# A hybrid encoder layer on one core: SSD moved under the pointwise and gated products, attention on its own

## The chip, the cores and the metric

One core of one Trainium2 chip. The metric is the device time of one execution in microseconds, the median of several runs. A profiled execution on the same chip gives the trace that is read below. Its engines are called PE (TensorE, matrix products), DVE (VectorE), ACT (ScalarE), POOL (GpSimd) and SP (SyncE, which issues nearly all DMAs).

## What is computed

One layer over 1088 tokens (1024 of a new stream, 64 of a running one), width 1024, all in float32. The input is normalised and projected; four mixers work on parts of the projection; their outputs are joined and projected back; a mixture of experts follows, and a last norm.

```python
def _layer(x, p, st, is_prompt):
    xn = _rmsnorm(x, p['g_mix'])
    proj = xn @ p['w_in']
    u_a, u_b, u_c, u_d = jnp.split(proj, [...], axis=-1)
    y_c, k_new, v_new = _band_attention_prompt(u_c, p['att_rel_bias'])   # or _sample, with a cache
    y_a, ssd_conv, ssd = _ssd_mixer(u_a, st['ssd_conv'], st['ssd'], p)   # a recurrence over tokens
    y_b, ccm_conv = _conv_module(u_b, st['ccm_conv'], p)                 # 31 taps, norm, pointwise product
    y_d, s5_re, s5_im = _s5_mixer(u_d, st['s5_re'], st['s5_im'], p)      # ends in ga * sigmoid(gb)
    mixed = jnp.concatenate([y_a, y_b, y_c, y_d], axis=-1) @ p['w_out']
    h = x + mixed
    return h + _hier_moe(_rmsnorm(h, p['g_ffn'])), ...                   # 32 experts, two for each token
```

## The kernel before, in words

The program is one list of instructions for each engine, in an order written out by hand; semaphores join them. An engine runs its list in order, so an instruction that waits holds up everything behind it on its engine. Tokens lie in 9 chunks of 128 (the last has 64). A float32 product runs as two passes through PE, so a product over one 512-column piece shows as two matmuls in the trace.

- **Projection** (`tile_part`, L603): 16 tiles of 128 output channels, two accumulators psA and psB in turn, 8 inner steps k. A pass covers 1088 tokens in the pieces of `CH` (L301): 512, 512 and 64, since a PSUM bank holds 512. ACT or DVE evacuates a finished tile into the arenas (L1123 to L1150, `gate_moved` L1376, `input_gated` L1430), each in one or two instructions. DVE meanwhile builds the S5 tables, takes the 31 and 4 taps of the convolutions (`tap`, L1482) and the S5 weights (L1528 to L1547). Between tiles 12 and 14 PE's list holds S5 steps (`S5_AT`, L399); the first, `w0`, waits for DVE's weights and for ACT's convolution activations.
- **S5 outputs** (`s5_output`, L670): for each of 16 groups one full product and two on one half of the 128 rows, all added in PSUM; then ACT's gelu, and a round trip through DRAM.
- **Norm of the convolution, v and dt** (L715 to L738), then the **pointwise products** (L741) and the **gated unit** (`glu`, L748): four whole tiles `gb0, gb1, ga0, ga1` of 1088 columns, moved by ACT (L1196 to L1204) and DVE (L1620). The sums of dt stand between them (L763).
- **Rounds of attention and SSD** (L892 to L912 on PE, L1276 on ACT, L1711 on DVE, L1961 on POOL): 9 rounds, each with one SSD chunk and two attention pairs (a pair is one chunk of queries and two heads, up to five key tiles). SSD of a chunk: `ssd_sums` (needs POOL's `ua`), ACT's exponential `ebc`, DVE's mask `dm`, ACT's decay, DVE's `ssd_operands` (`m`, `xdt`, `btok`, `ce`), PE's `ssd_outer`, DVE's `ssd_results` (`state`, `yd`), POOL's gate. Its accumulators all lie in psB, so that the sums of a chunk wait for the results of the one before. Attention uses psA for scores (`scores`, `scores_rest`), psC for turned probabilities and outputs; the fifth key tile has a place of its own in the order (`turn_rest`).
- **Back-projection** (`h_tile`, L917): 6 of 8 inner steps for chunks 0 and 1 first, with the SSD group sums (L817) after each half of chunk 1; ACT's logarithm and exponential and DVE's `group_norm` (L1683) follow, then the last two inner steps.
- **Routing and experts**: 21 blocks of gathered rows, weights streamed in by SP. Then a loop of 13 turns over spill groups on each engine (L561, L1037, L1346, L1901, L2012), each turn under an `If`; there are none with these inputs.
- **Final rows** (`summed`, `final_norm`, L1913 to L1928): `yrow` has three buffers, so row tile i waits until tile i - 3 has been written out (`s_yo`).

Of the kernel before, what the change touches and what calls it, by code (L numbers as in the profile page):

```python
# [15 lines left out]
ALU = mybir.AluOpType  # L16
# [4 lines left out]
P = 128  # L21
# [86 lines left out]
def encoder_step(nc, a, o):  # L108

    with ExitStack() as ctx:  # L110
# [35 lines left out]
        class Arena:  # L146
# [3 lines left out]
            def take(self, n):  # L150
# [19 lines left out]
        w_out = arena1[:, 2688:2688 + KT * D].rearrange("p (k n) -> p k n", k=KT)  # L170
# [20 lines left out]
        pts = a4.take(2 * BANDW)  # L191
# [25 lines left out]
              for x in [vtf[:, m * T:(m + 1) * T] for m in range(3)] + [arena4[:, 4608:4608 + T]]]  # L217
        w4 = Arena(arena1)
        ua, ebc, dm, ce = (w4.take(512).rearrange("p (h t) -> p h t", h=4) for _ in range(4))
# [17 lines left out]
        og = [[f1.take(D) for _ in range(2)] for _ in range(NT)]  # L237
        f3 = Arena(arena3)
        yrow = [f3.take(D) for _ in range(3)]
# [63 lines left out]

        s_params, s_hist, s_cache, s_bias = sem("params_in"), sem("histories_in"), sem("cache_in"), sem("bias_and_pointwise_in")
# [12 lines left out]
        s_yo, s_gfin = [sem(f"y_rows{k}_out") for k in range(3)], sem("g_final_in")  # L317
# [13 lines left out]
        dtp_pe = sem("dt_cumsums")  # L331
        cv_dve = sem("conv4_taps")
        cv_act = sem("conv4_silu")
        ssd_pe = steps("ssd_pe", "bc", "tr", "y", "st")
        ssd_act = steps("ssd_act", "ebc", "decay")
        ssd_dve = steps("ssd_dve", "dm", "m", "xdt", "btok", "ce", "state", "yd")
        ssd_pool = steps("ssd_pool", "ua", "xdd")
# [5 lines left out]
        cm_act = steps("ccm_act", "sq0", "sq1", "ln", "rs", "silu0", "silu1", "out0", "out1")  # L343
        cm_pe = steps("ccm_pe", "mu", "var", "pw0", "pw1")
        cm_dve = steps("ccm_dve", "cen0", "cen1", "n0", "n1")
        at_s, at_sa, at_t, at_tr, at_pv = (sem("att_scores"), sem("att_scores_rest0"), sem("att_probsT"),
                                           sem("att_probsT_rest"), sem("att_out"))
# [8 lines left out]
        glu_act = steps("glu_act", "sig0", "sig1")  # L356
        glu_pe = steps("glu_pe", "gb0", "gb1", "ga0", "ga1")
        glu_dve = sem("glu_dve")
# [69 lines left out]
        def pair_shape(p):  # L428

            i, pair = PAIRS[p]  # L430
            k0, tiles, b0 = band(i)
            five = len(tiles) > 4
            main = [list(range(len(tiles)))[:4], list(range(len(tiles)))[-4:]]
            rest = [4, 0] if five else None
            return i, pair, NTOK[i], k0, tiles, b0, main, rest

        def rests(p):
            return sum(pair_shape(n)[-1] is not None for n in range(p + 1))

        SCORES_AT = [0, 1024]  # L440

        @block.sync
        def _(sp):
# [57 lines left out]
            sp.wait_ge(glu_dve, 2)  # L501
            sp.dma_start(w_out, a["w_out"]).then_inc(s_wout, 16)
            sp.wait_ge(*ssd_dve.at(NT - 1, "state"))
# [57 lines left out]
            with sp.Fori(0, OVG) as i:  # L561
                with sp.If(groups > i):
                    for j in range(OVJ):
                        e = sp.value_load(spill_eid[0:1, ds(OVJ * i + j, 1)], min_val=0, max_val=E - 1)
                        sp.wait_ge(v_dn, OVJ * i + (j + 1))
                        sp.dma_start(wg[0], a["w_gate"][ds(e, 1), :, :].rearrange("o (p k) n -> (o p) k n", k=KT)
                                     ).then_inc(v_w, 16)
                        sp.dma_start(wu[0], a["w_up"][ds(e, 1), :, :].rearrange("o (p k) n -> (o p) k n", k=KT)
                                     ).then_inc(v_w, 16)
                        sp.dma_start(wd[0], a["w_down"][ds(e, 1), :, :].rearrange("o (p k) n -> (o p) k n", k=4)  # L570
                                     ).then_inc(v_w, 16)
# [6 lines left out]
            for i in range(NT):  # L578
                sp.wait_ge(f_dve_y, i + 1)
                dst = o["y_p"][tok(i), :] if i < NT - 1 else o["y_s"]  # L580
                sp.dma_start(dst, yrow[i % 3][0:NTOK[i], :]).then_inc(s_yo[i % 3], 16)
# [3 lines left out]
            for k in range(3):  # L585
                sp.wait_ge(s_yo[k], 16 * 3)

        @block.tensor
        def _(te):
# [13 lines left out]
            def tile_part(j, k):  # L603

                for lo, hi in CH:
                    if (j, k, lo) == (1, 0, TP):
# [63 lines left out]
            def s5_output(g, out):  # L670

                n, half = divmod(g, 2)
                rows = slice(half * 64, half * 64 + 64)
                te.matmul(out, mt[:, g].rearrange("p j c -> p (j c)"), u8[:, g, :], start=True, stop=False)
                for m in range(2):
                    mm = te.matmul(out, g8[m][rows, n].rearrange("p i c -> p (i c)"), hb[m][rows, n, :], start=False,
                                   stop=(m == 1))
# [24 lines left out]
            for g in range(6):  # L702
                at = 512 * (g % 2) + NS * (g // 2)
                mm = s5_output(g, psC[:, at:at + NS])
            mm.then_inc(*s5_pe.of("y0"))
            tile_moved(te, len(TILES) - 1)
            for g in (13, 15):
                mm = s5_output(g, psB[:, T + NS * (g // 2 - 6):T + NS * (g // 2 - 5)])
# [1428 lines left out]
```

## Time and profile before

| | us |
|---|---|
| median of 3 runs | 1341.45 (1341.34 to 1341.64) |
| the profiled execution | 1337.1 |
| its span, first to last instruction | 1335.3 |
| PE busy | 1165.3 |
| DVE busy | 443.1 |
| ACT busy | 230.9 |
| POOL busy | 68.7 |

The busy shares are means over stages with different limits: in the expert stage the DMA engines are full, in the projection PE is. The stages follow each other in time, so each is read by itself: the window row gives what its engines did, the timeline what waited for what. A bracket at the end of a timeline row gives the idle time ahead of the instruction and what ended it.

### The profile page before, as it was taken

Reading aid. Unit: us, or ns where it says so; the run is one execution under the profiler, and the core shown is the slowest. Engines: PE = TensorE matmul, PEld = TensorE weight load, DVE = VectorE, ACT = ScalarE, POOL = GpSimd, SP = SyncE. Lnnn points to the kernel's source line nnn. Section 1 sums busy time; section 2 is a strip of 40 time slices with the busy share of each in tenths; the row PEclk is TensorE's granted clock in tenths of the full one; section 3 lists DMA queues with packets and bytes.
Section 4 is the critical chain, followed back from the end, with each engine's and each line's share of the span. In section 5 each row is a group of like instructions: output and inputs, shape, how many; then the busy total and the mean of one; then the engine's idle time right before and its main releaser. Section 6 shows DMA issues by size and latency. Waiting matters only on the chain.

```text
span 1335.3 us, 17331 instructions
## 1 busy us (share of the span) xinstructions
PE 1165.3 (87%) x6967; PEld 537.2 (40%) x6967; DVE 443.1 (33%) x910; ACT 230.9 (17%) x437; POOL 68.7 (5%) x120
## 2 busy tenths in 40 slices
PE   6999999999977879799952799989998999998647
PEld 3555556567534544355522233333332333332212
DVE  3599985601165561211138001010010001010106
ACT  3300022014344442211110000000000001000003
POOL 0000000000011110000000000100100100100000
PEclk9999999999977887799975799999999999999969
DMA  6121131012030001112107989999999999899946
GB/s 260 32 89 48 49 69 29 1 55 67 18 126 1 1 0 52 48 51 71 61 8 261 399 313 414 415 411 413 413 411 414 413 399 401 316 406 413 369 181 240
DMA packets 71568, 271.69 MB, mean 203 GB/s; under 512 B 10432, under 2 KB 15232, under 8 KB 62912
## 3 DMA queue, kind: packets, MB, share of 16 engines
q1 hardware_dynamic: 65440, 252.73, 49.4%
q0 software_dynamic: 6048, 17.83, 3.4%
q8 instruction: 57, 0.93, 0.3%
q14 instruction: 23, 0.19, 0.0%
HBM read 251.17 MB, written 23.55 MB: 206 GB/s over the span
## 4 chain that ended last, share of the span: by engine, by line
PE 70%; DMA 10%; DVE 7%; SPq 7%; ACT 3%; issue 2%; POOLq 0%; DVEq 0%; ACTq 0%
PE psA L993 15%; PE psA L608 10%; PE psB L608 9%; PE psB L1018 8%; SPq L530 6%; DMA arena<-in_w_down 5%; PE psB L922 4%; PE psA L922 4%; DMA arena<-in_w_up 3%; PE psC L736 2%; PE psC L922 1%; PE psC L978 1%; PE psA L829 1%; PE psB L776 1%; DVE arena L1656 1%
## 5 line engine op out<-in xcount | busy, mean ns | idle before, releaser
L993 PE MATMUL psA<-arena 128*32 128x512 f32 x2688 | 304.1, 608 | 28.0 <-DMA arena<-in_w_up 26.2
L993 PEld LDWEIGHTS psA<-arena 128*32 128x32 f32 x2688 | 88.8, 112 | 227.3 <-issue 223.4
L1018 PE MATMUL psB<-arena 128*32 128x512 f32 x1344 | 151.5, 599 | 10.9 <-DMA arena<-in_w_down 10.9
L608 PE MATMUL psA<-arena 128*128 128x512 f32 (+1 forms) x384 | 129.3, 494 | 10.7 <-DVE arena L1371 10.7
L1876 DVE TENSOR_TENSOR arena<-psA,arena 128x512 f32<-128x512 f32 x21 | 14.5, 692 | 342.3 <-ACT arena L1324 342.3
L608 PE MATMUL psB<-arena 128*128 128x512 f32 (+1 forms) x384 | 126.1, 486 | 0.0
L608 PEld LDWEIGHTS psA<-arena 128*128 128x128 f32 x384 | 65.3, 194 | 73.6 <-issue 73.6
L1490 DVE SCALAR_TENSOR_TENSOR psC<-arena,params,psC 128x1024 f32<-128x1024 f32 x70 | 89.8, 1283 | 0.0
L608 PEld LDWEIGHTS psB<-arena 128*128 128x128 f32 x384 | 64.1, 191 | 61.7 <-issue 61.6
L1018 PEld LDWEIGHTS psB<-arena 128*32 128x32 f32 x1344 | 43.2, 110 | 103.7 <-issue 101.6
L1324 ACT ACTIVATE arena<-psA 128x512 f32<-128x512 f32 x21 | 12.5, 597 | 369.5 <-PE psA L993 369.5
L922 PE MATMUL psB<-arena 128*128 128x512 f32 (+1 forms) x128 | 58.6, 612 | 0.0
L1882 DVE COPY arena<-psB 128x512 f32<-128x512 f32 x21 | 14.5, 692 | 130.5 <-PE psB L1018 130.5
L922 PE MATMUL psA<-arena 128*128 128x512 f32 x128 | 56.7, 594 | 0.0
L1997 POOL DMA_INDIRECT expert_rows<-arena,ints x21 | 21.2, 1008 | 466.1 <-DVE arena L1882 466.1
L1336 ACT COPY arena<-psB 128x512 f32<-128x512 f32 x21 | 12.3, 585 | 169.4 <-PE psB L1018 169.4
L978 PE MATMUL psC<-mats,arena 128*128 128x128 f32 x168 | 25.1, 294 | 15.3 <-DMA arena<-hn_rows,ints 15.3
L922 PEld LDWEIGHTS psA<-arena 128*128 128x128 f32 x128 | 23.8, 190 | 27.3 <-issue 27.3
L922 PEld LDWEIGHTS psB<-arena 128*128 128x128 f32 (+1 forms) x128 | 22.8, 184 | 29.7 <-issue 29.6
L1990 POOL DMA_INDIRECT arena<-hn_rows,ints x21 | 21.5, 1025 | 254.5 <-DVE ints L1862 221.1
L978 PEld LDWEIGHTS psC<-mats,arena 128*128 128x128 f32 x168 | 20.9, 195 | 32.3 <-issue 28.9
L736 PE MATMUL psC<-arena 128*128 128x260 f32 (+1 forms) x144 | 32.1, 384 | 0.0
(400 smaller groups left out, 1130.8 us busy)
## 6 DMA issues: line engine op xcount, KB each, us to landing
arena<-in_w_gate SPq DMA_DIRECT2D x128, 512.0 KB, 12.3
arena<-in_w_up SPq DMA_DIRECT2D x128, 512.0 KB, 16.2
arena<-in_w_down SPq DMA_DIRECT2D x64, 1024.0 KB, 18.0
arena<-in_w_cm SPq DMA_DIRECT2D x16, 512.0 KB, 3.7
arena<-expert_rows SPq DMA_DIRECT2D x16, 512.0 KB, 10.6
arena<-in_xT SPq DMA_DIRECT2D x8, 544.0 KB, 9.2
arena<-in_w_out SPq DMA_DIRECT2D x1, 4096.0 KB, 12.1
arena<-in_x_rows SPq DMA_DIRECT2D x8, 512.0 KB, 4.4
```

Of the source, the lines that this page charges most:

```text
L530: sp.dma_start(w[:, ks, :], src[ds(e, 1), :, :].rearrange("o (p k) n -> (o p) k n", k=KT)[:, ks, :]).then_inc(s_wgu[r][c], 16)
L608: mm = te.matmul(AB[j % 2][:, lo:hi], wring[:, j % 4, k * P:(k + 1) * P], xn[:, k, lo:hi], start=(k == 0), stop=(k == KT - 1))
L736: mm = te.matmul(psC[0:NTOK[i], 512 * (i % 2):512 * (i % 2) + VD], xn[:, k, tok(i)], wvd[:, k, :], start=(k == 0), stop=(k == KT - 1))
L922: mm = te.matmul(hps[i][0:NTOK[i], n * 512:(n + 1) * 512], mix[:, k, tok(i)], w_out[:, k, n * 512:(n + 1) * 512], start=(k == CA), stop=(k ...
L978: mm = te.transpose(psC[:, k * P:(k + 1) * P], xg.rearrange("p (m k) -> p k m", k=KT)[:, k, :], ident)
L993: mm = te.matmul(psA[tile, at:at + FF], xgT[:, k, tile], w[o % RG][:, k, :], start=(k == 0), stop=(k == KT - 1))
L1018: mm = te.matmul(psB[tile, n * 512:(n + 1) * 512], hT[:, k * P + c * TW:k * P + c * TW + TW], wd[o % RD][:, k, n * 512:(n + 1) * 512], sta ...
L1490: ins = ve.scalar_tensor_tensor(out=dst if t == width - 1 else acc, in0=x[:, at + t:at + t + n], scalar=w(t), in1=acc, op0=ALU.mult, op1=A ...
L1876: ve.tensor_tensor(hmid, psA[:, FF:2 * FF], actg, ALU.mult).then_inc(m_hm, 1)
L1882: ve.tensor_copy(orow[q % 2][:, 512:1024], psB[:, 512:1024]).then_inc(m_dnD, 1)
L1990: po.indirect_dma_start(xg, None, hn_dram, bass.IndirectOffsetOnAxis(ap=slot_in[:, q:q + 1], axis=0), bounds_check=last_in, oob_is_err=Fal ...
L1997: po.indirect_dma_start(out_dram, bass.IndirectOffsetOnAxis(ap=slot_out[:, q:q + 1], axis=0), orow[q % 2], None, bounds_check=last_out, oo ...
```

## The change

- The projection's pieces are 368, 360 and 360 columns (`CHT`), one in each bank; evacuations go in three or four cuts (`CUTS`).
- `s5_outputs` takes two groups together: their two full products, then the half-row products, even and odd in turn.
- Pointwise products and gated unit become 18 units of three, three and two eighths of the tokens (`UNITS6`: `gb`, `pw`, `ga`), in the three banks of psA. SSD runs beside them: psB holds its sums and inner products, psC its outputs and states, `dm` and `ce` have two buffers, and each chunk is followed by one unit. The dt sums come after the sixth unit.
- Attention starts when SSD and the units are done: each round does the scores of pair p + 2, turns the probabilities of p + 1 and takes the outputs of p. The heads' scores lie in psA and psB, outputs in psA's third bank, the turned fifth tile in psB's third; `pts` has two buffers.
- ACT squares the gated SSD output in attention rounds 1 and 2; the group sums stand ahead of the halves of `h_tile(0)`.
- The spill loop stands under one `If(groups > 0)` on each engine.
- `yrow[i]` is the buffer of the gathered expert rows, `og[i][0]`, and nothing waits for `s_yo` until the end.

The diff, cut to its core:

```diff
-        w_out = arena1[:, 2688:2688 + KT * D].rearrange("p (k n) -> p k n", k=KT)
+        w_out = arena1[:, 3712:3712 + KT * D].rearrange("p (k n) -> p k n", k=KT)
-        pts = a4.take(2 * BANDW)
+        pts = [a4.take(2 * BANDW), vbf[:, 0:2 * BANDW]]
+        dm, ce = [dm0, dm1], [ce0, ce1]
+        yrow = [og[i][0] for i in range(NT)]
+        GLU = [(0, 3), (3, 6), (6, 8)]
+        UNITS6 = [(kind, m, n) for kind in ("gb", "pw", "ga") for m in range(2) for n in range(3)]
+        CHT = [(0, 368), (368, 728), (728, T)]
+        CUTS = [(0, 368, 0), (368, 728, 512), (728, TP, 1024), (TP, T, 1024 + TP - 728)]
...
             def tile_part(j, k):
-                for lo, hi in CH:
+                for b, (lo, hi) in enumerate(CHT):
...
-                    mm = te.matmul(AB[j % 2][:, lo:hi], wring[:, j % 4, k * P:(k + 1) * P], xn[:, k, lo:hi],
+                    mm = te.matmul(AB[j % 2][:, 512 * b:512 * b + hi - lo], wring[:, j % 4, k * P:(k + 1) * P], xn[:, k, lo:hi],
...
-            def s5_output(g, out):
+            def s5_outputs(g, even, odd):
+                n = g // 2
+                for x, out in ((g, even), (g + 1, odd)):
+                    te.matmul(out, mt[:, x].rearrange("p j c -> p (j c)"), u8[:, x, :], start=True, stop=False)
                 for m in range(2):
+                    for half, out in ((0, even), (1, odd)):
+                        rows = slice(half * 64, half * 64 + 64)
+                        mm = te.matmul(out, g8[m][rows, n].rearrange("p i c -> p (i c)"), hb[m][rows, n, :],
+                                       start=False, stop=(m == 1))
...
+            for u in range(6):
+                unit(u)
+            ssd_inner(0)
             te.wait_ge(*dtp_dve.at(0, "a"))
...
+            ssd_sums(0)
+            unit(6)
+            unit(7)
+            ssd_sums(1)
+            unit(8)
+            for c in range(NT):
+                ssd_outer(c)
+                if c + 1 < NT:
+                    ssd_inner(c + 1)
+                if c + 2 < NT:
+                    ssd_sums(c + 2)
+                unit(9 + c)
...
+            te.wait_ge(glu_dve, 6)
+            te.wait_ge(*ssd_dve.at(NT - 1, "m"))
+            te.wait_ge(*ssd_res.at(NT - 1, "yd"))
+            for p in range(-2, NPAIR):
                 if p + 2 < NPAIR:
                     scores(p + 2)
...
+                if 0 <= p + 1 < NPAIR:
+                    turn_probs(p + 1)
                 if p >= 0:
                     outputs(p)
...
             for n in range(2):
+                group_sums(n)
                 h_tile(0, n, Z_LAST[:6])
             for n in range(2):
                 h_tile(1, n, Z_LAST[:6])
-                group_sums(n)
...
+            for c in range(NT):
+                ssd_masked(c)
+                if c:
+                    ssd_results(c - 1)
+                ssd_operands(c)
+                if c >= 4:
+                    unit_gated(c - 4)
+            ssd_results(NT - 1)
+            unit_gated(5)
...
+            for p in range(-2, NPAIR):
+                if p + 2 < NPAIR:
+                    probs(p + 2, 0)
+                    probs(p + 2, 1)
                 if p >= 0:
                     move_output(p)
+                if 0 <= p + 1 < NPAIR:
                     move_probs(p + 1, 0)
                     move_probs(p + 1, 1)
+                    move_rest(p + 1)
+                if p in (1, 2):
+                    group_squares(p - 1)
...
+            with po.If(groups > 0):
+                with po.Fori(0, OVG) as i:
+                    with po.If(groups > i):
...
-                if i >= 3:
-                    ve.wait_ge(s_yo[i % 3], 16 * (i // 3))
-                ve.scalar_tensor_tensor(out=yrow[i % 3][0:M, :], in0=fin[i % 3][0:M, 0:D], scalar=hrs[0:M, i:i + 1],
+                ve.scalar_tensor_tensor(out=yrow[i][0:M, :], in0=fin[i % 3][0:M, 0:D], scalar=hrs[0:M, i:i + 1],
```

## Rows read from the trace of the kernel before

**Rows 1.** Windows: stretch, its us, engines PE PEld DVE ACT POOL, clock, DMA.

```profile
430.00:507.00 77.00, 63.79 (x481) 39.01 (x479) 46.65 (x132) 36.16 (x99) 11.71 (x18) 0.83 0.00 1
...
745.00:1274.00 529.00, 489.31 (x4276) 162.95 (x4276) 55.39 (x81) 37.13 (x63) 39.71 (x40) 0.98 0.98 392
```

**Rows 2.** Chain that ended last: start, us, engine, tile, line, count.

```profile
192.03 15.52 PE psB L608 x48
...
588.06 6.87 PE psA L922 x16
```

**Rows 3.** Timelines of DVE and PE, projection: start, us, instruction, idle before.

```profile
83.49 1.23 DVE L1434 TENSOR_TENSOR arena<-psB,arena 128x1024 f32<-128x1024 f32 x1 [1.17 <-PE psB L608]
...
209.39 1.23 DVE L1532 TENSOR_TENSOR arena<-arena 128x1024 f32<-128x1024 f32 x1
...
213.21 1.04 PE L630 MATMUL psC<-mats,arena 128*128 128x128 f32 x8
```

**Rows 4.** Timeline of PE: one S5 output group, then SSD's half-row products.

```profile
283.56 0.73 PE L676 MATMUL psC<-arena 64*128 64x136 f32 x4
284.22 0.50 PE L674 MATMUL psC<-arena 128*128 128x136 f32 x2
284.65 0.73 PE L676 MATMUL psC<-arena 64*128 64x136 f32 x4
...
387.34 0.49 PE L784 MATMUL psB<-arena 64*128 64x128 f32 x4
```

**Rows 5.** Chain, then ACT's timeline, where the v/dt products end.

```profile
340.25 4.02 PE psA L744 x12
...
345.21 0.20 ACT L1195 ACTIVATE small<-params 128x4 f32<-128x4 f32 x1
```

**Rows 6.** Timelines of DVE and POOL: gated unit, then SSD work of mixed rounds.

```profile
361.13 2.20 DVE L1623 SCALAR_TENSOR_TENSOR arena<-psA,params,arena 128x1088 f32<-128x1088 f32 x1 [3.60 <-PE psA L752]
...
379.67 2.04 DVE L1656 TENSOR_TENSOR arena<-arena 64x256 f32<-64x256 f32 x2
...
380.21 1.22 POOL L1965 TENSOR_TENSOR arena<-mats,small 128x512 f32<-128x512 f32 x1
...
434.84 0.69 DVE L1633 TENSOR_TENSOR arena<-psB,mats 128x512 f32<-128x512 f32 x1
...
442.11 0.74 DVE L1643 TENSOR_TENSOR arena<-arena,psB 128x256 f32<-128x256 f32 x2
...
443.30 1.45 DVE L1656 TENSOR_TENSOR arena<-arena 64x256 f32<-64x256 f32 x2
446.26 0.97 DVE L1672 SCALAR_TENSOR_TENSOR small<-small,psB 64x64 f32<-64x64 f32 x4 [1.51 <-PE psB L807]
447.26 0.61 DVE L1678 SCALAR_TENSOR_TENSOR arena<-arena,params,psB 128x128 f32<-128x128 f32 x2
```

**Rows 7.** Timeline of PE: one mixed round, with one full attention pair.

```profile
428.07 0.66 PE L800 MATMUL psB<-arena 128*64 128x128 f32 x8 [3.40 <-DVE arena L1656]
...
437.33 1.13 PE L829 MATMUL psA<-arena 64*128 64x512 f32 x4
...
440.63 1.15 PE L857 MATMUL psC<-mats,arena 128*128 128x128 f32 x8
444.81 0.66 PE L800 MATMUL psB<-arena 128*64 128x128 f32 x8 [3.02 <-DVE arena L1656]
...
446.14 2.04 PE L829 MATMUL psA<-arena 64*128 64x512 f32 x4
```

**Rows 8.** Timeline of PE, back-projection.

```profile
509.41 13.07 PE L922 MATMUL psC<-arena 128*128 128x512 f32 x24
...
542.94 6.51 PE L922 MATMUL psC<-arena 128*128 128x512 f32 x8 [6.33 <-DVE arena L1685]
```

**Rows 9.** The end: SP's waits (us, times, longest), then PE's timeline.

```profile
SPq L576 <- POOLq L2027: 7.4, 1, 7.4
...
1316.97 3.67 PE L1072 MATMUL psA<-arena 128*128 128x512 f32 x8 [2.03 <-DVE arena L1927]
```

More of the change, by code:

```diff
@@ L218, in encoder_step @@
         w4 = Arena(arena1)
-        ua, ebc, dm, ce = (w4.take(512).rearrange("p (h t) -> p h t", h=4) for _ in range(4))
+        ua, ebc, dm0, dm1, ce0, ce1 = (w4.take(512).rearrange("p (h t) -> p h t", h=4) for _ in range(6))
+        dm, ce = [dm0, dm1], [ce0, ce1]
         xdt = w4.take(256)
@@ L431, in pair_shape @@
             k0, tiles, b0 = band(i)
[L432 to L435, printed above, removed]
+            return i, pair, NTOK[i], k0, tiles, b0, min(len(tiles), 4), len(tiles) > 4
         def rests(p):
-            return sum(pair_shape(n)[-1] is not None for n in range(p + 1))
-        SCORES_AT = [0, 1024]
+            return sum(pair_shape(n)[-1] for n in range(p + 1))
+        HEAD_PS = [psA, psB]
         @block.sync
@@ L584, in _ @@
             sp.wait_ge(s_gfin, 16)
-            for k in range(3):
-                sp.wait_ge(s_yo[k], 16 * 3)
+            sp.wait_ge(s_yo, 16 * NT)
         @block.tensor
@@ L791, in ssd_outer @@
[L791 to L809 removed]
+            te.matmul(psC[:, 544:548], ones[L8, :], aa[L8, 8, :], start=True, stop=True).then_inc(*cm_pe.of("dt"))
@@ L821, in scores @@
             def scores(p):
-                i, pair, nq, k0, tiles, _, main, rest = pair_shape(p)
+                i, pair, nq, k0, tiles, _, n, rest = pair_shape(p)
                 if p:
                     te.wait_ge(at_max, 2 * p)
-                for h in range(2):
-                    rows = slice(h * 64, h * 64 + 64)
-                    lo, n = main[h][0] * P, sum(tiles[m][1] for m in main[h])
-                    mm = te.matmul(psA[0:nq, SCORES_AT[h]:SCORES_AT[h] + n], mix[rows, Q + pair, tok(i)],
-                                   kt[rows, pair, k0 + lo:k0 + lo + n], start=True, stop=True)
@@ L831, in scores @@
[L831 to L844 removed]
+                for lo, hi in ((0, n * P), (4 * P, 4 * P + tiles[-1][1]))[:1 + rest]:
+                    for h in range(2):
+                        rows = slice(h * 64, h * 64 + 64)
+                        mm = te.matmul(HEAD_PS[h][0:nq, lo:hi], mix[rows, Q + pair, tok(i)],
+                                       kt[rows, pair, k0 + lo:k0 + hi], start=True, stop=True)
@@ L1689, in biased @@
             def biased(p, h):
-                i, pair, nq, _, tiles, b0, _, rest = pair_shape(p)
-                nk, at = sum(w for _, w in tiles), SCORES_AT[h] - (P if h and rest else 0)
+                i, pair, nq, _, tiles, b0, _, _ = pair_shape(p)
+                nk = sum(w for _, w in tiles)
                 ve.wait_ge(at_s, p + 1)
-                ve.tensor_tensor_reduce(sc[p % 2][h][0:nq, 0:nk], psA[0:nq, at:at + nk],
+                ve.tensor_tensor_reduce(sc[p % 2][h][0:nq, 0:nk], HEAD_PS[h][0:nq, 0:nk],
                                         bias[0:nq, 2 * pair + h, b0:b0 + nk], -1.0, -NEG, ALU.add, ALU.min,
```

590 lines of the change are left out of this document (272 added, 318 removed).

## The prediction

> **What bounds the kernel now.** I read the windows by stage first, then the chain of waits in order of time, then the timelines of the stages that the change touches. The expert stage keeps the DMA engines 98% busy for 529 us [rows 1]; the change leaves it alone, so it only starts earlier or later, and what is won ahead of it counts in full. Ahead of it three things are to be seen. The projection is one unbroken run of TensorE (PE): 15.52 us for each tile of 48 passes [rows 2]. The rounds that mix attention with SSD have no engine that is full: in 77 us PE is busy 63.8, VectorE (DVE) 46.7, ScalarE (ACT) 36.2, at a mean granted clock of 0.83 [rows 1]; PE waits about 3 us in each round for DVE's SSD operands, and the passes behind that wait run at the lower clock (four score passes 2.04 us, against 1.13 us at the upper one) [rows 7]. Behind the rounds PE waits 6.33 us for the normalised SSD output [rows 8]; at the end everything waits for POOL's loop over spill groups that don't occur [rows 9].
>
> The profiled execution took 1337.1 us (span 1335.3), 4.35 below the median 1341.45. I sum in its times and add 4.35.
>
> **1. Projection in thirds: -5.3 us.** A pass over 1088 columns takes 15.52/16 = 970 ns. Sixteen 512-column passes take 6.87 us [rows 2], 0.84 ns a column, so 1088 columns are worth 912 ns; the remaining 58 ns is the 64-column piece, which costs far more than its columns. Pieces of 368, 360 and 360 have no such short one: 58 ns x 16 = 0.93 us a tile, 14.8 us for 16. Most of it isn't kept. PE comes to the first S5 transposes (tile 12, k = 3) 12.4 x 0.93 = 11.5 us earlier, at 201.7 instead of 213.21. They need DVE's weights, ready at 209.39 + 1.23 = 210.6 [rows 3]. That DVE chain waited for the projection for only 1.17 us, at 83.49 [rows 3]; before that it hangs on tile 1. Two tiles give it 1.9 us, the wait of 1.17 goes, since tile 3 comes 3.7 earlier, and evacuating in three or four cuts costs it some 0.6: 2.4 us. So PE waits at 208.2 for some 6.5 us, which is 4.9 us earlier than now. After a wait as long (6.33 us) eight 512-column passes took 6.51 us instead of 3.4 [rows 8]: 3 us lost at the lower clock. The 3.6 tiles behind keep 3.4 us: -4.9 + 3.0 - 3.4 = -5.3. Bounds: -8.3 without the clock loss, -3 if ACT's extra cuts, queued ahead of the convolution's activations that DVE awaits, delay DVE by 2 us; -14.8 if DVE weren't late.
>
> **2. S5 outputs in pairs: -5.4 us.** Now two full passes (284.22 to 284.65, 0.43 us) and four on one row half (283.56 to 284.22, 0.66 us) make a group, 2.18 us a pair [rows 4]. Four passes that alternate between the halves, at 387.34, show 0.49 us with the last one's tail, where four on one half show 0.73 for their 0.66 [rows 4]: 0.42, so eight take 0.84; four full passes take 0.43 + 0.24, since the change of shape is paid once. 1.51 against 2.18, x 8 pairs = -5.4. If alternation gives nothing, eight halves stay at 1.32: -1.5. If both halves ran wholly side by side: -10.
>
> **3. SSD under the products: 73 us.** From the last v/dt product (340.25) to the end of the first chunk's back-projection (542.94 + 6.51) is 209.2 us now [rows 5, 8]. After the change this stretch is SSD with 18 units, then attention, then the w_out products.
> Lead: three units fill psA; the fourth waits for ACT, which is busy with dt until 345.41 [rows 5] and has the sigmoid's table to load; units 3 to 5, chunk sums, exponentials and mask follow: 19.5 us to the first finished operand.
> Rounds: DVE is the widest engine. Mask 0.69; ce 1.45; state and output 446.26 to 447.87, 1.6; masked product, xdt, btok 442.11 to 443.30, 1.2 [rows 6]: 4.9 us, and PE's and ACT's work of a chunk lies beside it. ce has both inputs in SBUF, and where POOL ran the sum operand beside it, it took 2.04 instead of 1.45 [rows 6]; in the packed rounds it always does: 5.5 us. Eight rounds make 44 us. A gated unit costs DVE 2.20 us for 1088 columns [rows 6], 0.8 for a third, and four of them lie in the rounds: 3 us. The last chunk's outputs and gate take 4, restarts of the clock 2.5: 73 us. Bounds 66 (ce at 1.45, full clock) and 85.
> The Trainium skill, "SBUF — State Buffer", section "Who interferes with whom", says that a DVE instruction with two SBUF inputs and a GpSimd one that reads SBUF exclude each other for a whole instruction, which speaks against packing these rounds. By it ce could cost a whole sum operand (1.22 us) over 1.45, where the row lost 0.59; the sum would be 5 us longer, inside the bounds.
>
> **4. Attention alone: 77 us.** One full pair is in PE's row of 437.33 to 441.78: scores, remainder, outputs and turned probabilities, 4.45 us without a wait [rows 7]. DVE and ACT have less per pair, since a mixed round of two pairs takes 16.7 us (428.07 to 444.81) [rows 7], and 77 us of them hold DVE busy 46.7 and ACT 36.2, SSD included [rows 1]: 10.1 and 7.8 a round, less SSD's 4.9 and some 2: 2.6 and 2.9 a pair. Probabilities are now turned a round ahead of the outputs, and pts has two buffers, so I let PE bound it: 10 full pairs x 4.45 = 44.5; 8 shorter ones about 2.5 each, 20; filling and draining 8; 4.5 for the lower clock while the short pairs leave PE idle. Bounds 69 and 95, the latter if each pair keeps 1 us of hand-over.
>
> **5. Products behind it: 28.4 us.** Group sums now stand ahead of the w_out products, with ACT's logarithms, exponentials and DVE's norm under three quarters of them. 56 passes of 512 columns at 0.43 = 24, 12 passes of group sums 2 x 1.94, 0.6 of hand-overs. The 6.33 us wait [rows 8] has no successor: x rows and w_out are loaded long before. Stretch: 73 + 77 + 28.4 = 178.4 against 209.2: **-30.8 us**.
>
> **6. End: -9.2 us.** SP waited 7.4 us for POOL, which went through its 13 empty turns [rows 9]. One branch replaces them: -7.0 (bounds -5.5, -7.4). The Trainium skill, "Runtime: NRT & Kernel Launch", section "Instruction fetch mechanics", says that a taken branch to a far target fetches instructions first; by it part of this would come back, but no row prices one such fetch. Rows in place remove DVE's wait for the first y rows and PE's 2.03 behind it [rows 9]: -2.2; the gathered rows, issued ahead, are in by then. If they aren't, 0.
>
> Sum: -5.3 - 5.4 - 30.8 - 9.2 = -50.7; 1337.1 - 50.7 + 4.35 = **1290.75 us**; I say 1291.
>
> **Rivals.**
> Nothing won by splitting (chance 0.20): SSD and attention alone take what the mixed rounds took, 340.25 to 509.41, 169 us [rows 5, 8], because each alone is a chain of hand-overs between PE, ACT and DVE. For: the mixed rounds leave every engine idle. Against: PE's 4.45 us of a pair hold no wait. Then the stretch gives only 40.0 - 28.4 = 11.6: 1310.
> Best packing (0.13): SSD 66, attention 69, and DVE not late in the projection: the stretch gives 15 more and the projection 9.5: 1266.
> Lower clock throughout (0.05), the one on the other side: without SSD beside it PE has too many small gaps, and the clock stays at 1.2 GHz, its lower level. PE is then the bound: SSD 9.2 us a round and 104 in all, attention 2 x 4.45 a pair and 121 in all: 75 us more than 150. It decides from 68% of that time at the lower level (50.7 of 75 us); wholly so: 1366. For: the 0.83 of the mixed rounds [rows 1]. Against: passes behind continuous work run at the upper level [rows 7].
> Thirds that shorten nothing, if the 58 ns is a cost of each instruction: 1296, inside the range.
>
> **How the numbers follow.** Forecast 0.62, no gain by splitting 0.20, best packing 0.13, lower clock 0.05. Range 1272 to 1312: the bounds of terms 3 and 4 carry it, with both middle rivals at its edges. Faster by over 0.2% (about what can be told from no change here) 0.94, same 0.01, slower 0.05.
>
> **What would show it.** Term 1: 14.6 us a tile, and a PE wait of some 6 us before the first S5 transposes; without that wait, DVE was not late. Term 2: 12 us between the last projection pass and the convolution's mean. Term 3: first scores 73 us after the last v/dt product, DVE nearly full, ce at 2 us. Term 4: full pairs every 4.5 us with PE full; 5.5 or more means hand-overs. Term 5: no PE wait ahead of the last two steps of the back-projection's first chunk. Term 6: POOL's signal within 1 us of the last scatter's landing, no wait on y rows. A granted clock under 0.8 in the two middle stages would make the forecast wrong.

## The result

The changed kernel takes **1266.58 us** (median of 4 runs, 1263.78 to 1270.35) against 1341.39 us (median of 4), a ratio of **0.945** (95% interval 0.9436 to 0.9468). The direction was forecast, the size was not: 1266.6 lies 5.4 us below the range of 1272 to 1312. Its profiled execution took 1266.7 us (span 1264.9), so here nothing has to be added to come from the profiled run to the median; 4.35 us of the forecast's distance are that addition.

The chain of waits of the changed kernel, in order of time (start, us, engine, tile, line, count), answers to [rows 2, 5, 8, 9]: the last projection tile, the mean of the convolution, the last v/dt product, the first chunk's back-projection, the first expert product, the last scatter, the first final rows.

```profile
265.40 14.63 PE psB L611 x48
290.43 4.02 PE psB L726 x12
312.36 17.75 PE psC L741 x80
481.33 3.45 PE psC L910 x8
680.81 16.64 PE psA L982 x128
1212.15 4.39 DMA expert_rows<-arena,ints
1223.08 6.57 PE psA L1062 x8
```

Between them, and with the first scores (393.55) and the first sums behind attention (456.61) from PE's timeline, the stages are:

| stage | before, us | forecast | after, us | difference |
|---|---|---|---|---|
| start to the last projection pass | 283.4 | 278.1 | 280.0 | -3.3 |
| S5 outputs | 17.2 | 11.8 | 10.4 | -6.8 |
| mean, v, dt, variance | 39.7 | 39.7 | 39.7 | 0 |
| last v/dt product to the first scores (SSD, units) | | 73 | 63.4 | |
| attention | | 77 | 63.1 | |
| products to the end of the first chunk | | 28.4 | 28.2 | |
| these three together | 209.2 | 178.4 | 154.7 | -54.5 |
| routing, to the first expert product | 195.9 | 195.9 | 196.0 | +0.1 |
| experts, to the landing of the last scatter | 532.9 | 532.9 | 535.7 | +2.8 |
| end | 57.0 | 47.8 | 48.4 | -8.7 |

The sum is -70.4, where -50.7 was forecast. The miss of 19.7 us is SSD (9.6) and attention (13.9); the other rows differ from the forecast by less than 3 us each and take back 3.8. Windows of the two stages (columns: stretch, its us, PE, PEld, DVE, ACT, POOL, clock, DMA share, GB/s), to be held against [rows 1]:

```profile
330.10:393.55 63.45, 56.77 (x333) 31.36 (x334) 43.79 (x130) 30.61 (x69) 22.79 (x37) 0.97 0.03 10
393.55:456.60 63.05, 57.20 (x532) 38.61 (x533) 45.08 (x144) 49.14 (x139) 0.00 (x0) 0.95 0.18 70
```

PE is busy for 90% of both and its clock stays at the upper level but for a few us. In the kernel before the same work (units, SSD and attention, 340.25 to 509.40) held 32 us of idle PE time and a clock of 0.81 in the mixed rounds:

```profile
340.25:367.30 27.05, 24.72 (x81) 13.00 (x81) 5.54 (x8) 12.48 (x16) 1.03 (x1) 1.00 0.06 22
367.30:509.40 142.10, 112.16 (x785) 65.30 (x785) 84.86 (x256) 65.11 (x185) 22.51 (x33) 0.81 0.08 30
```

PE's timeline shows how little the SSD rounds of the changed kernel wait. A round with a wide unit (408 columns) takes 4.97 us, and all eight together, 350.34 to 389.95, take 39.6 us with 2.2 us of waits, over half of them in the last:

```profile
354.28 0.44 PE L799 MATMUL psC<-arena 128*64 128x128 f32 x4
...
359.25 0.44 PE L799 MATMUL psC<-arena 128*64 128x128 f32 x4
...
364.06 0.44 PE L799 MATMUL psC<-arena 128*64 128x128 f32 x4 [0.22 <-DVE arena L1660]
...
389.95 0.34 PE L799 MATMUL psC<-arena 128*64 128x64 f32 x4 [1.18 <-DVE arena L1660]
```

### The profile page after: what moved, and what is told of

It reads as the page before. It is cut to its first block, busy times and chain, and to the rows that moved or that the text cites. A ratio compares the mean times of both kernels' runs of the same rounds, so it can differ in the third digit from the quotient of the medians.

```text
span 1264.9 us, 17121 instructions
## 1 busy us (share of the span) xinstructions
PE 1123.9 (89%) x6967; PEld 544.3 (43%) x6967; DVE 440.7 (35%) x922; ACT 232.3 (18%) x471; POOL 67.4 (5%) x120
## 4 chain that ended last, share of the span: by engine, by line
PE 57%; DVE 18%; DMA 11%; SPq 7%; ACT 4%; issue 2%; POOL 0%; POOLq 0%; DVEq 0%; ACTq 0%
PE psA L982 14%; PE psB L1007 8%; DVE psC L1490 7%; SPq L533 6%; DMA arena<-in_w_down 6%; PE psB L910 5%; PE psA L910 4%; PE psA L611 3%; DMA arena<-in_w_up 3%; PE psC L741 3%; PE psB L611 2%; DMA arena<-hn_rows,ints 2%; PE psC L967 1%; DVE arena L1490 1%; PE psA L763 1%
## 5 line engine op out<-in xcount | busy, mean ns | idle before, releaser
L982 PE MATMUL psA<-arena 128*32 128x512 f32 x2688 | 308.4, 615 | 26.2 <-DMA arena<-in_w_up 24.5
L611 PE MATMUL psA<-arena 128*128 128x360 f32 (+1 forms) x384 | 124.7, 483 | 10.7 <-DVE arena L1367 10.7
L611 PE MATMUL psB<-arena 128*128 128x360 f32 (+1 forms) x384 | 120.3, 472 | 0.0
L611 PEld LDWEIGHTS psA<-arena 128*128 128x128 f32 x384 | 74.8, 197 | 55.0 <-issue 14.1
L611 PEld LDWEIGHTS psB<-arena 128*128 128x128 f32 x384 | 73.4, 192 | 44.2 <-issue 1.7
L1319 ACT ACTIVATE arena<-psA 128x512 f32<-128x512 f32 x21 | 12.5, 597 | 372.3 <-PE psA L982 372.3
L910 PE MATMUL psB<-arena 128*128 128x512 f32 (+1 forms) x128 | 59.4, 619 | 0.0
L910 PEld LDWEIGHTS psA<-arena 128*128 128x128 f32 x128 | 23.9, 190 | 27.7 <-issue 27.7
```

The costliest lines, as they stand in the source:

```text
L611: mm = te.matmul(AB[j % 2][:, 512 * b:512 * b + hi - lo], wring[:, j % 4, k * P:(k + 1) * P], xn[:, k, lo:hi], start=(k == 0), stop=(k == ...
L910: mm = te.matmul(hps[i][0:NTOK[i], n * 512:(n + 1) * 512], mix[:, k, tok(i)], w_out[:, k, n * 512:(n + 1) * 512], start=(k == CA), stop=(k ...
L982: mm = te.matmul(psA[tile, at:at + FF], xgT[:, k, tile], w[o % RG][:, k, :], start=(k == 0), stop=(k == KT - 1))
```

## Experiments

The first theory after the result: the two terms were too long because (a) in the forecast `ce` was taken to meet POOL in every round, which its new place prevents, and (b) a pair of attention was costed by the old order. The rivals: SSD's length comes from PE alone, wherever `ce` stands; and the separation itself, not the order inside the stages, made the gain.

### ce behind btok again

```diff
 def ssd_masked(c):        # ce no longer here
-    for g in range(2): ... ce[c % 2] ...
 def ssd_operands(c):
     ve.tensor_copy(btok[0:L, :], ...)
+    for g in range(2): ... ce[c % 2] ...
     ve.wait_ge(*ssd_act.at(c, "decay"))
```

> The changed kernel with one edit: ce is made behind btok again, as in the kernel before, not directly behind the mask. The SSD stage, from the end of the last v/dt product (330.11) to the first scores (393.55), takes 63.4 us in the changed kernel, its eight rounds of outputs (350.34 to 389.95) 39.6. First theory: the 5.5 us a round of the forecast was wrong because the new place keeps ce clear of POOL's sum operand (ce 0.84 to 1.20 us instead of 1.45 to 2.04). Then ce goes back to 1.45 to 2.04 us, DVE needs 4.75 to 5.35 us a round without a gated unit and 0.8 more with one, and the eight rounds take 42 to 46 us. Rival: DVE has slack and PE's own 4.97 us sets the round wherever ce stands: at most 40.5 us.

One run took 1281.45 us. The eight rounds, from the first chunk's outputs at 350.86 to the last's at 403.86, take 53.0 us, 13.4 more than with `ce` early. The theory gave 42 to 46, so it had the direction right and the size too small. The timelines of DVE, POOL and PE in one round of this kernel (start, us, instruction, idle before):

```profile
367.35 0.61 POOL L1975 TENSOR_TENSOR arena<-arena,small 128x256 f32<-128x256 f32 x1 [4.14 <-DVE arena L1648]
367.38 2.04 DVE L1654 TENSOR_TENSOR arena<-arena 64x256 f32<-64x256 f32 x2
367.92 1.22 POOL L1958 TENSOR_TENSOR arena<-mats,small 128x512 f32<-128x512 f32 x1
...
370.26 0.44 PE L799 MATMUL psC<-arena 128*64 128x128 f32 x4 [2.31 <-DVE arena L1660]
```

`ce` starts with POOL's decayed input and ends 0.28 us behind POOL's sum operand; PE waits 2.31 us. In DVE's and POOL's timelines of the changed kernel, where `ce` stands behind the mask, it reads

```profile
358.83 1.04 POOL L1958 TENSOR_TENSOR arena<-mats,small 128x512 f32<-128x512 f32 x1
359.56 1.19 DVE L1643 TENSOR_TENSOR arena<-arena 64x256 f32<-64x256 f32 x2
359.83 1.19 POOL L1964 TENSOR_TENSOR arena<-arena 128x128 f32<-128x128 f32 x2
...
370.54 0.83 DVE L1643 TENSOR_TENSOR arena<-arena 64x256 f32<-64x256 f32 x2
```

1.19 us where it meets the last 0.3 us of the sum operand and then the gate, 0.83 where POOL is idle. So the place of `ce` is worth 13.4 us of this stage; the rival (at most 40.5 us) falls.

### ce late, POOL behind it

```diff
-                po.wait_ge(*ssd_dve.at(c, "xdt"))
+                po.wait_ge(*ssd_dve.at(c, "ce"))
```

> The changed kernel with ce late, behind btok, and with one more edit: POOL waits for ce of a chunk before it makes that chunk's decayed input, so that neither that nor the next sum operand runs beside ce. With ce late alone, ce takes 2.04 us in most rounds and the eight rounds 53.0 us (6.9 us each in the full ones). If ce is long because POOL's instructions hold it up, it falls to 0.84 us and the rounds lose 0.5 to 1.2 us each (44 to 49 us in all), although POOL's work now starts later. If ce's place in the chain is what costs, and its length is its own, ce stays at 1.45 us or more and the rounds get longer than 6.9 us by POOL's delay.

From the timelines of DVE and PE of this kernel:

```profile
364.94 0.84 DVE L1654 TENSOR_TENSOR arena<-arena 64x256 f32<-64x256 f32 x2
...
366.62 0.44 PE L799 MATMUL psC<-arena 128*64 128x128 f32 x4 [1.11 <-DVE arena L1660]
...
395.03 0.34 PE L799 MATMUL psC<-arena 128*64 128x64 f32 x4 [1.65 <-DVE arena L1660]
```

`ce` takes 0.84 us in all eight full rounds, and these take 44.2 us (350.82 to 395.03); the run took 1270.65 us. Of the 13.4 us, 8.8 are POOL's instructions holding up DVE's, and 4.6 (44.2 against 39.6) the later place in the chain, with whatever POOL's later start costs. How POOL holds `ce` up can be read from its two DVE instructions in the round with `ce` late shown above (durations in ns, starts in us):

```profile
L1654 DVE TENSOR_TENSOR arena<-arena x2: 856/1013/1170, 367.4 to 368.3; 64x256 f32<-64x256 f32 x2
```

The first ends at 368.24, 0.28 us behind the decayed input (367.96), the second at 369.42, 0.28 us behind the sum operand (369.14); the two take 0.84 us together with POOL out of the way. The row of 1.45 that the forecast used [rows 6] stands beside POOL as well: in the kernel before POOL's decayed input runs from 443.26 to 443.87 and its gate from 443.84.

### ce early in the kernel before

```diff
 def ssd_masked(c):
+    for g in range(2): ... ce ...
 def ssd_operands(c):
-    for g in range(2): ... ce ...
 def ssd_outer(c):
-    te.wait_ge(*ssd_dve.at(c, "ce"))
+    te.wait_ge(*ssd_dve.at(c, "btok"))
```

> The kernel before with one edit: ce is made directly behind the mask, as in the changed kernel, and PE's outer products wait for btok. The mixed rounds take 142 us; PE waits about 3 us in each for ce, the last of the SSD operands, and with ce late in the changed kernel its SSD rounds grew from 39.6 to 53 us. If the place of ce is what made SSD expensive in the mixed rounds too, the operands end 1.5 to 2 us earlier in each round and the rounds lose 8 to 14 us: 1326 to 1333 us. If the mixing itself sets the rounds (each engine's list holds two attention pairs ahead of the next SSD step), ce's new place moves less than 3 us and the gain needed the separation.

**1316.27 us** (4 runs, 1314.58 to 1319.36), a ratio of 0.983 (0.9803 to 0.9851) to the kernel before. PE's timeline over one mixed round, as in [rows 7]:

```profile
431.20 0.66 PE L800 MATMUL psB<-arena 128*64 128x128 f32 x8 [1.65 <-DVE arena L1658]
444.99 0.66 PE L800 MATMUL psB<-arena 128*64 128x128 f32 x8 [1.65 <-DVE arena L1658]
```

The window from the first scores to the first w_out product (columns as above):

```profile
368.19:484.16 115.97, 98.40 (x785) 58.47 (x785) 77.75 (x256) 65.23 (x185) 19.74 (x33) 0.91 0.09 37
```

The round falls from 16.7 to 13.8 us, PE's wait from 3.0 to 1.65, the clock rises from 0.81 to 0.91, and all rounds take 116.0 instead of 142.1 us. That is more than the expected 8 to 14: besides 1.4 us of waiting, each round gets back PE time, since passes behind a shorter wait run at the upper clock more often (PE busy 98.4 us instead of 112.2 for the same 785 records). One move of two DVE instructions is worth 26 us of this stage without any separation; the changed kernel's whole stretch gained 54.5.

### The old order of attention, alone

All SSD steps are left out of the rounds of the kernel before.

> The kernel before without any SSD step in its rounds (sums, mask, operands, outputs, states, gates are left out, so what SSD adds to the output is missing); the rounds hold attention alone in the old order. The mixed rounds take 142 us from the first scores to the first w_out product, attention alone in the changed kernel 63.1. If the old order of attention is as good as the new one and the long rounds came from SSD's chain alone, this takes 63 to 70 us. If the old order (probabilities turned one pair ahead at most, one buffer for them, the fifth tile in a step of its own) has hand-overs of its own, it takes 85 to 110 us, and a good part of the gain is the new order of attention, not the separation.

Attention in the old order runs from 368.60 to 441.09. The window, then PE's timeline at the first instruction of three full pairs:

```profile
368.60:441.09 72.49, 67.12 (x533) 42.80 (x533) 43.81 (x144) 49.11 (x141) 0.00 (x0) 0.91 0.15 61
```

```profile
399.30 1.13 PE L828 MATMUL psA<-arena 64*128 64x512 f32 x4 [0.65 <-DVE small L1683]
...
403.69 1.13 PE L828 MATMUL psA<-arena 64*128 64x512 f32 x4
...
408.33 1.13 PE L828 MATMUL psA<-arena 64*128 64x512 f32 x4 [0.19 <-DVE small L1683]
```

72.5 us lies between the two expectations, nearer to the first: PE is nearly full with a pair every 4.4 to 4.6 us. Between full pairs the old order waits 0.19 us at every second one; the 0.65 us and others like it stand ahead of the first full pair and between the short ones. So SSD's steps added 142.1 - 72.5 = 69.6 us to the mixed rounds, and the new order is worth 9.4 us (72.5 against 63.1): 6.1 in the ten full pairs, the rest around them, where part of it is the clock (0.91 against 0.95 over the stage). The whole took 1457.91 us in one run, which says nothing of attention: without SSD's part the tokens are routed otherwise, and PE goes through spill groups.

### Scores head by head

```diff
-                for lo, hi in ((0, n * P), (4 * P, ...))[:1 + rest]:
-                    for h in range(2):
+                for h in range(2):
+                    for lo, hi in ((0, n * P), (4 * P, ...))[:1 + rest]:
```

> The changed kernel with one edit: PE makes all scores of one head and then those of the other; in the changed kernel the wide pieces of both heads stand side by side and then the two narrow ones. A full pair takes 3.90 us there (428.86 to 432.76), the forecast had 4.45. First theory: passes on different row halves run side by side, so the order of the pieces is worth 0.5 us a full pair: pairs of 4.4 us, attention (63.1 us) 5 us longer. Rival: the 0.55 us came from turning the fifth tile together with the others and from fewer changes of shape, not from the scores: less than 0.1 us a pair, attention within 1 us.

Nothing changed: 1264.73 us in one run, 63.0 us of attention (394.24 to 457.28), and a full pair still 3.9 us, here 425.62 to 429.51, in the changed kernel 428.86 to 432.76. PE's timeline of that pair in the changed kernel:

```profile
428.86 0.69 PE L851 MATMUL psA<-arena 64*128 64x512 f32 x1
428.87 0.69 PE L851 MATMUL psB<-arena 64*128 64x512 f32 x1
...
430.28 1.09 PE L863 MATMUL psC<-mats,arena 128*128 128x128 f32 x8
431.21 0.38 PE L870 MATMUL psB<-mats,arena 128*128 128x128 f32 x2
431.52 1.31 PE L885 MATMUL psA<-arena 128*64 128x128 f32 x20
```

The two heads' passes start 0.01 us apart and run side by side, whatever their order. The rival holds. By the rows, the old order's fifth tile (second and fourth instruction of a pair, with a turned tile between them) costs 0.31 + 0.41 us of scores where the new one adds 0.46, and turning takes 0.37 + 1.09 where it now takes 1.24; that this is the cause was read, not tried.

### S5 halves one after the other

```diff
-                for m in range(2):
-                    for half, out in ((0, even), (1, odd)):
+                for half, out in ((0, even), (1, odd)):
+                    for m in range(2):
```

> The changed kernel with one edit: of the eight half-row passes of two S5 groups the four of the even half come first and then the four of the odd half, not in turn. In the changed kernel such a pair of groups takes 1.33 us (279.86 to 281.08 and so on), the forecast had 1.51. If it is the alternation that lets the halves run side by side, the eight passes go back from 0.66 to 1.32 us a pair and the eight pairs take 5.3 us more (16 instead of 10.5 us from the last projection pass to the mean of the convolution). If, as the scores by head suggest, passes on different halves overlap whatever their order as long as no full pass stands between them, at most 0.5 us more.

The same again: 10.55 us from 279.22 to 289.77 (10.5 with alternation), 1265.56 us in one run. What pays is that eight half-row passes stand together without a full pass between them: they take 0.66 us, side by side, where the kernel before needed 1.32 [rows 4]. No run put a full pass back between them in this kernel, so that part rests on the rows of the kernel before.

### The 64-column piece again

```diff
-        CHT = [(0, 368), (368, 728), (728, T)]
-        CUTS = [(0, 368, 0), (368, 728, 512), (728, TP, 1024), (TP, T, 1024 + TP - 728)]
+        CHT = CH
+        CUTS = [(0, TP, 0), (TP, T, 1024)]
```

> The changed kernel with one edit: the projection in pieces of 512, 512 and 64 columns again, evacuated in two cuts. By the forecast a tile goes back from 14.63 to 15.52 us, PE comes to the S5 transposes at about 213, where DVE's weights are ready, so there is no wait and no lower clock behind it: the last projection pass ends at 283.4 instead of 280.03, 3.3 us later, though 14.2 us of passes are added. Rival: the wait is PE's own doing in another way (ACT's or DVE's extra cuts delay the convolution): then DVE's weights come earlier than 207.2 by more than 1 us with two cuts.

The S5 transposes start at 213.31 without a wait; DVE's weights are ready at 210.73, 3.5 us later than with the extra cuts (207.23), so the rival falls. The last projection pass ends at 284.97, 4.9 us later instead of 3.3; one run took 1273.08 us. 1.7 us of that come from one stretch at a clock of 0.68 (226.7 to 232.0), of which more below; the other 3.2 us are what was expected. The thirds as built keep 3 to 5 us of the 14.2 us of passes that they spare.

### S5 steps three inner steps later

```diff
-        S5_AT = {(12, 3): "w0", (12, 5): "w1", (12, 7): "col", (13, 1): "mt0", (13, 3): "mt1", (13, 5): "x0", ...
+        S5_AT = {(12, 6): "w0", (13, 0): "w1", (13, 2): "col", (13, 4): "mt0", (13, 6): "mt1", (14, 0): "x0", ...
```

> The changed kernel with one edit: the eight S5 steps between the last projection tiles stand three inner steps later. In the changed kernel PE waits 6.07 us for DVE's S5 weights (207.27) and then runs 5.8 us slower than the passes of the kernel before would allow, at a granted clock of 0.93 over 208 to 280. If DVE's lateness alone keeps the gain of the thirds away, the wait falls to about 0.7 us, the clock stays up, the last projection pass ends at 267 to 269 instead of 280.03, DVE's S5 scans end before that (28 us behind the first state products, at about 262), and the whole gains 11 to 12 us. Rival: S5's own chain becomes the bound, since its states come later in the tile order; then PE waits ahead of the S5 outputs and the whole gains less than 4 us.

**1258.02 us** (4 runs, 1254.72 to 1259.74), ratio 0.939 (0.9376 to 0.9412). PE's timeline, the changed kernel first, then this one:

```profile
207.27 1.97 PE L633 MATMUL psC<-mats,arena 128*128 128x128 f32 x8 [6.07 <-DVE arena L1532]
```

```profile
207.74 1.09 PE L633 MATMUL psC<-mats,arena 128*128 128x128 f32 x8 [0.55 <-DVE arena L1532]
...
254.68 14.79 PE L611 MATMUL psB<-arena 128*128 128x368 f32 x48
269.31 0.63 PE L677 MATMUL psC<-arena 128*128 128x136 f32 x4
```

The transposes start 0.5 us later, but PE has done three inner steps more by then, and the clock stays up. The projection ends at 269.3, 14.0 us before that of the kernel before: nearly all of the 14.8 us that the thirds can spare. The S5 outputs wait for nothing. DVE's lateness was what kept the gain away. Of the expected 11 to 12 us the whole gains 8.6 by the medians (1266.58 to 1258.02), and 12.0 between the two profiled executions, of which this kernel's is its fastest run.

### Both, with one table load less

```diff
             ac.activation(dta, dta, ACT.Exp, scale=-1.0)...
+            ac.activation(aexp, col("a_log", 0, 4), ACT.Exp)...
             ac.wait_ge(*dtp_act.at(0, "e"))
             ac.activation(dta, dta, ACT.Ln, bias=col("one"))...
-            ac.activation(aexp, col("a_log", 0, 4), ACT.Exp)...
```

> The edit of the S5 steps three inner steps later, and ACT takes the exponential of the SSD parameters directly behind that of dt, ahead of the logarithm, which spares one table load (1.28 us in the rows) ahead of the first sigmoid. Expected: the gain of the first edit plus 1.3 us, if the fourth unit's wait for ACT (3.27 us at 337.22) sets the lead of the SSD stage: 1253 to 1255 us. Rival: the first SSD operands hang on dt's sums, not on the sigmoids, and the table load was covered: the same time as with the first edit alone.

**1253.00 us** (5 runs, 1251.89 to 1255.39), ratio 0.936 (0.9339 to 0.9372): faster than both kernels. The wait of the fourth unit for ACT falls by the length of the load:

```profile
324.68 3.92 PE L763 MATMUL psA<-arena 128*128 128x408 f32 x12 [1.99 <-ACT arena L1196]
```

and the first outputs follow the last v/dt product by 17.3 us, where the first edit alone has 18.5. Against that edit the median falls by 5.0 us, more than the expected 1.3; the two profiled executions differ by 1.7, and the rest isn't explained. In them 0.6 us was lost again in attention (63.7 against 63.0 us).

### POOL's gates behind the rounds

```diff
                 if c + 2 < NT:
                     sum_operand(c + 2)
-                if c:
-                    gated_output(c - 1)
-            gated_output(NT - 1)
+            for c in range(NT):
+                gated_output(c)
```

> The changed kernel with one edit: POOL multiplies all nine gated outputs behind its last sum operand and decayed input, not one in each round. In the changed kernel ce takes 0.84 us where POOL is idle beside it and 1.20 where the gated output runs beside it. If that contention is on the path, ce is 0.84 us in every round and the eight rounds lose up to 0.36 us each, 37 us instead of 39.6. If PE's passes (4.97 us in rounds with a wide unit) set the round, only the rounds with a gated unit on DVE (5.9 us) get shorter: 0.5 to 1 us in all, and up to 1 us of it is lost again because the squares of the group norm wait for the gates.

The rounds take 39.45 us instead of 39.6 (350.69 to 390.14). `ce` takes 0.83 to 0.85 us in most of them and 1.03 in the three in which it still meets the end of the sum operand, so what POOL adds to `ce` in its new place is hidden behind PE's 4.97 us. Once `ce` is out of the way, PE sets the rounds. Attention takes 64.8 us (393.74 to 458.54) instead of 63.1, and the whole 1267.73 in one run. The expected reason, squares that wait for the gates, isn't it: POOL is done at 396.96, and the first square begins at 403.94. DVE's first scaling of probabilities runs beside POOL's gates and is 1.28 us longer than in the changed kernel (last row):

```profile
390.14 6.82 POOL L1964 TENSOR_TENSOR arena<-arena 128x128 f32<-128x128 f32 x18
395.48 1.57 DVE L1718 TENSOR_SCALAR arena<-arena,small 128x128 f32<-128x128 f32 x1
```

```profile
395.29 0.29 DVE L1718 TENSOR_SCALAR arena<-arena,small 128x128 f32<-128x128 f32 x1
```

### Group sums behind the second chunk

```diff
             for n in range(2):
-                group_sums(n)
                 h_tile(0, n, Z_LAST[:6])
             for n in range(2):
                 h_tile(1, n, Z_LAST[:6])
+                group_sums(n)
```

> The changed kernel with one edit: the group sums stand behind the two halves of the second chunk again, as before. The forecast priced the new place at 6.33 us, the wait of PE for the normalised SSD output. If so, the wait returns, and the products from the end of attention to the end of the first chunk (456.61 to 484.6, 28.0 us) take 33 to 37 us, the passes behind the wait included. Rival: the squares of the gated output, now taken in attention rounds 1 and 2, were the late part before, and the sums' place is worth less than 1 us.

PE's timeline of this kernel, as in [rows 8]:

```profile
458.43 13.49 PE L910 MATMUL psC<-arena 128*128 128x512 f32 x24 [0.36 <-issue]
...
492.37 6.74 PE L910 MATMUL psC<-arena 128*128 128x512 f32 x8 [6.33 <-DVE arena L1698]
```

The wait of 6.33 us is back to the hundredth, though the squares are still taken early, so the rival falls; eight passes behind the wait take 6.74 instead of 3.45. The products take 40.7 us (458.43 to 499.1), 12.5 more, where 33 to 37 were expected; the run took 1277.81 us. The wait and the passes behind it make 9.6 of the 12.5. The other 3 are 24 passes at the start, 13.3 us instead of 10.4: the clock is 0.55 from 458.4 to 465 here and 1.00 from 456 to 470 in the changed kernel. Whether that follows from the order of the sums isn't shown.

### Empty turns again

The branch around the spill loop is taken out on all five engines.

> The changed kernel without the branch around the spill loop: 13 empty turns on each engine again, the final rows still in place. Forecast of the step: 7.0 us between the last scatter's landing and the first gathered rows' DMA (bounds 5.5 and 7.4). The changed kernel takes 1.3 us there (1216.5 to 1217.9). Rival: the branch itself costs (instructions fetched behind it), so that the difference is under 5.5 us.

Two rows of this kernel's chain, the last scatter and the first DMA of gathered rows:

```profile
1207.91 6.00 DMA expert_rows<-arena,ints
...
1222.69 0.33 SPq L579
```

and the first DMA in the changed kernel's:

```profile
1217.88 0.34 SPq L580
```

From the landing at 1213.9 to SP's first DMA it takes 8.8 us, in the changed kernel 1.3 (1216.54 to 1217.88): 7.4 us, the upper bound. One run took 1270.94 us. The branch itself costs nothing that shows.

## Why the forecast missed

- **Projection (-5.3, measured -3.3): right in mechanism.** PE came to the transposes at 201.2 (201.7 forecast), waited 6.07 us (6.5) and went on at 207.27 (208.2). The term for the lower clock was mis-sized: 5.6 us instead of 3, 2.2 behind the wait and 3.4 in a second stretch around 222 to 230 that the forecast had no row for. That DVE's lateness cost the rest was shown by moving the S5 steps. A tile takes 14.63 us with three pieces, as many as before, so the 58 ns was the short piece and not a cost of each instruction.
- **S5 outputs (-5.4, measured -6.8): right, mis-sized.** Eight half passes take 0.66 us, not 0.84: the halves run wholly side by side. The forecast's bound for that case, -10, was worked out wrong: eight pairs of 1.33 instead of 2.18 us give -6.8.
- **SSD (73, measured 63.4): the step that failed.** "In the packed rounds it always does: 5.5 us" was wrong twice. The price of `ce` without POOL was taken as 1.45 us from [rows 6], but that row stands beside POOL too; alone it is 0.84. And the change moves `ce` from behind `btok` into `ssd_masked`, behind the mask (the cut diff doesn't show this line), where it starts when the sum operand is nearly or wholly done; the forecast priced it as meeting the whole of it. With `ce` left late the stage takes 13.4 us more, with POOL kept off it 4.6. The rounds came out at 39.6 instead of 47 with the gated units, since PE (4.97 us with a wide unit, 2.2 us of waits in all eight) and not DVE sets them. The lead was right (20.2 for 19.5); the last chunk took 3.6 where 4 and 2.5 were allowed.
- **Attention (77, measured 63.1): the second that failed.** 4.45 us was a true price of a full pair in the old order (4.4 to 4.6 in the run without SSD), but the new order takes 3.90: 5.5 us. That the fifth tile's place makes the 0.55 us of a pair was read from rows, not tried. The rest was allowance: 32.5 us for short pairs, filling and clock, where 24.1 were needed (63.1 - 39.0), and 27.4 even in the old order (72.5 - 10 x 4.51).
- **Products (28.4, measured 28.2) and end (-9.2, measured -8.7): right.** The order of the group sums and the branch were confirmed by undoing them; the rows in place were only read (final tiles of 3.43 us with no wait for the rows written out).
- **Experts: 2.8 us more**, which the forecast did not have; the kernel before varies by as much between runs (1337.7 to 1341.6), so no cause is claimed.
- **The range.** Its lower end, 1272, rested on bounds of 66 and 69 us that used the same two rows as the forecast; both stages came out below their bounds. The rival of best packing gave the right time, 1266, by luck: DVE was late in the projection after all, 11.5 us more than this rival had, while the two stages came out 8.5 us under its 66 and 69, and the 4.35 us added for the median weren't needed. The lower clock throughout did not come: 0.97 and 0.95. That splitting wins nothing did not come true, but the move of `ce` in the kernel before brings 23 of the 75 us without it. What the separation alone is worth was not tried by itself; if effects measured in different kernels may be added, the moved `ce` (26.1) and the group sums (12.5, with 3 us of clock) taken off the 54.5 us leave 16, of which the new attention order explains 9.4.

## What to carry to other kernels

Before a duration from a trace is used as the price of an instruction, look at what ran beside it on the other engines; the bound below it is a row without that neighbour. When a change moves an instruction inside one engine's list, price the old list with only that move first: here it was nearly a third of the gain. When a faster stage meets a late producer, move the consumers in the order by as much as the producer is late.

## What the hardware showed

- `ce` is two DVE products with both inputs in SBUF. Together they took 0.84 us with POOL idle, 1.45 and 2.04 beside POOL's decayed input (0.61 us) and what POOL did next. In the round shown above each ends 0.28 us behind a POOL instruction. The Trainium skill, "SBUF — State Buffer", section "Who interferes with whom", says that a DVE instruction with two SBUF inputs contends with a GpSimd instruction that reads SBUF. These rows agree; the forecast's row of 0.59 lost, which seemed to speak against a hold-up of a whole instruction, compared two contended rows.
- A DVE scaling of 128x128 values in SBUF took 1.57 us beside POOL's gates and 0.29 with POOL idle, in one place of one run.
- Passes on the two row halves of PE overlap fully whether they alternate or come four and four (0.66 us for eight passes of 136 columns both ways).
- The clock fell without a wait just ahead of it. In the changed kernel PE is busy in every us of 222 to 230, and the granted clock is 0.57, mostly its lower level of 1.2 GHz; ahead of it stand 32 passes of 32 columns of the S5 steps. With the 64-column piece the stretch at 226.7 to 232.0 shows 0.68 in the same place; with the S5 steps later, and in the kernel before (1.00 from 223 to 230), the same passes are followed by none. Why stays open. The window of the changed kernel:

```profile
222.00:230.00 8.00, 8.00 (x20) 5.21 (x20) 0.00 (x0) 1.64 (x5) 0.00 (x0) 0.57 0.01 2
```
